# Queries and keys projected with dimensions on partitions, and heads gathered by SBUF transfers, in a hybrid attention layer

## What is computed

```python
h = einsum('bnd,de->bne', x, w_in)             # 1024 -> 3328 columns
qa, ka, va, ga, qb, kb, vb, gb = split(h)      # 512 each, but kb and vb 128
qa, ka = rope(qa), rope(ka)                    # mixer A: 8 heads, 1-D rotary
out_a = dilated_attention(qa, ka, va) * silu(ga)   # mask with multiplicities 0 to 3
qb = axial_rope(rms_norm_heads(qb, q_norm))    # mixer B: 8 query heads,
kb = axial_rope(rms_norm_heads(kb, k_norm))    # 2 key/value heads, 2-D rotary
out_b = softmax(qb @ kb.T * scale) @ vb * silu(gb)
f = concat(out_a, out_b) @ w_out
y = layer_norm(alpha * x + f) * ln_g + ln_b
```

## Time and profile before

| | |
|---|---|
| three runs | 474.97, 476.57, 477.52 us; median 476.57 |
| profiled execution, first to last instruction | 474.6 us |
| PE busy | 438.0 us, 92% |
| DVE, POOL, ACT busy | 301.4, 248.1, 230.7 us |
| DMA | 30.00 MB, mean 63 GB/s |

### The profile page before, as it was taken

One profiled execution on the slowest core, in us unless ns is written; L12 is line 12 of the kernel. 1 busy time (PEld: TensorE's weight loads), 2 busy tenths in 40 slices (PEclk: granted clock), 3 DMA queues, 4 the chain that ended last, 5 costly groups with the idle time before them and its releaser, 6 DMA issues.

```text
span 474.6 us, 8965 instructions
## 1 busy us (share of the span) xinstructions
PE 438.0 (92%) x3292; PEld 413.2 (87%) x3292; DVE 301.4 (64%) x826; ACT 230.7 (49%) x519; POOL 248.1 (52%) x340
## 2 busy tenths in 40 slices
PE   1999979998899999999999999999999789999990
PEld 1999969987799999998899999999888678999990
DVE  1543675339987788664577877855586777433664
ACT  3332113335456565666565565655675876121222
POOL 1126953795554746334346565653543773454664
PEclk9999989999899999999999999999999989999997
DMA  6611212110200101102010010110200136231222
GB/s 237 255 45 52 71 35 74 39 46 23 68 23 23 46 23 36 56 24 66 14 54 23 24 46 24 40 51 23 68 1 23 44 111 245 88 95 42 78 100 89
DMA packets 23291, 30.00 MB, mean 63 GB/s; under 512 B 1872, under 2 KB 19408, under 8 KB 23248
## 3 DMA queue, kind: packets, MB, share of 16 engines
q1 hardware_dynamic: 22816, 29.30, 19.0%
q10 hardware_dynamic: 432, 0.13, 0.1%
HBM read 26.28 MB, written 3.15 MB: 62 GB/s over the span
## 4 chain that ended last, share of the span: by engine, by line
PE 66%; POOL 10%; DVE 10%; issue 7%; ACT 3%; DMA 2%; SPq 1%; ACTq 0%; DVEq 0%; POOLq 0%
PE bank L504 15%; PE bank L505 15%; PE bank L506 15%; PE bank L465 9%; PE bank L593 6%; POOL scr L1062 3%; DVE prob L870 2%; PE bank L551 2%; PE bank L552 2%; DMA h<-x_prompt 2%; DVE tmp_s L796 1%; POOL tanh L1048 1%; ACT prob L707 1%; DVE p_lo L878 1%; POOL w_lo L1032 1%
## 5 line engine op out<-in xcount | busy, mean ns | idle before, releaser
L504 PE MATMUL bank<-w_hi,t_lo 128*128 128x256 f32 x576 | 168.2, 292 | 1.9 <-DVE nmax L870 0.8
L506 PE MATMUL bank<-w_hi,t_hi 128*128 128x256 f32 x576 | 164.0, 285 | 0.0
L505 PE MATMUL bank<-w_lo,t_hi 128*128 128x256 f32 x576 | 163.9, 285 | 0.0
L504 PEld LDWEIGHTS bank<-w_hi,t_lo 128*128 128x128 f32 x576 | 111.5, 194 | 3.1 <-DVE nmax L870 1.0
L505 PEld LDWEIGHTS bank<-w_lo,t_hi 128*128 128x128 f32 x576 | 111.6, 194 | 0.1
L506 PEld LDWEIGHTS bank<-w_hi,t_hi 128*128 128x128 f32 x576 | 111.3, 193 | 0.0
L1032 POOL TENSOR_TENSOR w_lo<-raw,w_hi 128x512 fp32r<-128x512 f32 x52 | 67.2, 1302 | 59.2 <-ACT w_hi L659 59.1
L1113 POOL TENSOR_SCALAR prob<-prob,den 128x512 f32<-128x512 f32 (+1 forms) x96 | 60.5, 635 | 68.6 <-DVE den L899 68.5
L707 ACT ACTIVATE prob<-prob,nmax 128x512 f32<-128x512 f32 (+1 forms) x96 | 62.3, 649 | 54.1 <-DVE nmax L870 53.6
L878 DVE TENSOR_TENSOR p_lo<-bank,p_hi 128x512 fp32r<-128x512 f32 x80 | 54.8, 685 | 3.0 <-ACT p_hi L716 2.2
L659 ACT ACTIVATE w_hi<-raw 128x512 fp32r<-128x512 f32 x62 | 37.6, 622 | 34.6 <-DMA raw<-w_in 17.4
(11 more groups left out here) (97 smaller groups left out, 784.3 us busy)
## 6 DMA issues: line engine op xcount, KB each, us to landing
raw<-w_in SPq DMA_DIRECT2D x50, 256.0 KB, 2.8
raw<-w_out SPq DMA_DIRECT2D x16, 256.0 KB, 2.9
h<-x_prompt SPq DMA_DIRECT2D x7, 512.0 KB, 6.8
h<-x_sample SPq DMA_DIRECT2D x4, 512.0 KB, 9.6
y_prompt<-h SPq DMA_DIRECT2D x8, 256.0 KB, 2.1
y_sample<-h SPq DMA_DIRECT2D x4, 256.0 KB, 2.1
cst<-consts SPq DMA_DIRECT2D x1, 960.0 KB, 9.5
h<-x_prompt SPq DMA_DIRECT2D x2, 256.0 KB, 3.8
```

Source lines behind the costliest of these rows:

```text
L504: nc.tensor.matmul(out, a_lo, b_hi, start=(m == 0), stop=False)
L505: nc.tensor.matmul(out, a_hi, b_lo, start=False, stop=False)
L506: ins = nc.tensor.matmul(out, a_hi, b_hi, start=False, stop=(m == KT - 1))
```

## The change

The layout of the data is redone on the host: x comes a second time, transposed (`xt`), the columns of `w_in` are permuted into 12 chunks and `w_out` into slices of one dimension block by 512 columns, all contiguous per partition. The first chunk (`START`) has 512 columns, the keys and queries of A's heads 0 to 3; the other 11 have 256.

- x is loaded transposed, 384 KB for a dimension block. There are no `x_transposes`.
- `start` projects the first chunk dimension block by dimension block, with six PSUM banks open, the weights stationary and the tokens streamed (512 and 256).
- Items are now 48 products of 256 columns (values and B's keys, two token tiles) or, for gates, B's queries and A's keys and queries, 24 of 512 columns (`n` = 0, 1) or 48 of 256 (`n` = 2).
- Queries and A's keys lie with dimensions on partitions, the first halves of four heads in one bank, the second halves in another. DVE multiplies by cosines and sines, POOL subtracts and adds two blocks of 768, ACT rounds 1536 columns, DVE takes the remainder.
- Each head is then gathered from these 32-partition pieces by DMAs from SBUF to SBUF: 4 for the queries of a head, 8 for its keys, 96 KB each. The per-head PE transposes are gone, but for 6 blocks of B's keys.
- B's queries get their RMS factor in `mask_max`; the sums of squares come from 24 products of 4 columns (`square_sums`).
- The output projection has 2 halves of 512 columns. Head order is A 0-3, B 0-7, A 4-7. Items end at step 64, 21 (block, tile) pairs of the output projection lie in steps 70 to 81, and 7 ring places hold the weights.

```diff
-ORDER = [10, 8, 11, 9, 12, 0, 2, 4, 6, 1, 3, 5, 7]
-BESIDE = ((0, 5), (3, 8), (55, 44), (62, 50), (65, 52), (72, 54))
+BESIDE = ([(c, n) for c in range(C_GA0, C_QB0 + 1) for n in range(3)] + [(KEYS_T, 0), (KEYS_T, 1)] +
+          [(c, n) for c in range(C_GB0, C_GA1 + 1) for n in range(3)])
+PACE = ((0, 0), (15, 9), (16, 11), (34, 17), (43, 20), (55, 29), (64, 32))
+WIDE_AT = {70: 0, 71: 1, 72: 2, 73: 3, 74: 4, 76: 5, 81: 6}
...
+                for n, src in enumerate((high[rows, 0], high[rows, 1], low[rows, 0], low[rows, 1])):
+                    sp.dma_start(q_st[32 * n:32 * n + 32, j % 4, :].bitcast(F32), src).then_inc(q_staged[j % 4], 16)
...
+                for part, src in enumerate((high, low)):
+                    for n in range(4):
+                        sp.dma_start(ka_st[32 * n:32 * n + 32, part, slot, :].bitcast(F32), src[rows, n % 2]) \
+                            .then_inc(ka_staged[slot], 16)
...
+            load_chunk(C_GA0)
+            sp.wait_ge(rot_lo, 1)
+            stage_keys(0)
+            sp.wait_ge(rot_lo, 2)
+            stage_query(0, "q")
+            for j in range(1, 4):
+                stage_keys(j)
+                stage_query(j, "q")
...
+            for c in range(C_VKB, C_QB1 + 1):
+                load_chunk(c)
...
+                for k in range(KT):
+                    pe.wait_ge(w_hi_done, k + 1)
+                    pe.wait_ge(x_hi, k + 1)
+                    for group in range(2):
+                        one(group, k, w_hi, t_hi, k == 0, False)
+                    pe.wait_ge(x_lo, k + 1)
...
+                nc.gpsimd.tensor_tensor(low[:, 0], low[:, 0], high[:, 1], ALU.subtract)
+                nc.gpsimd.tensor_tensor(low[:, 1], low[:, 1], high[:, 0], ALU.add).then_inc(rotated_done, 1)
```

More of the change, by code:

```diff
@@ L77 @@
+C_VA, C_GA0, C_VKB, C_QB0, C_GB0, C_QB1, C_GB1, C_KA1, C_VA1, C_QA1, C_GA1 = range(1, 12)
+KEYS_T = "keys"
+GATE_AT = {C_GA0: 0, C_GB0: 4, C_GB1: 6, C_GA1: 2}
+SLICE_W = 512
+SLICES_OF = [len(cols) * KT // SLICE_W for _, cols in CHUNKS]
+FIRST_SLICE = [sum(SLICES_OF[:c]) for c in range(len(CHUNKS) + 1)]
+IN_SLICES = FIRST_SLICE[-1]
+OUT_HALVES = D_MODEL // SLICE_W
+OUT_SLICES = OUT_HALVES * KT
+RING, RAW = 7, 2
+HEADS = N_HEADS_A + N_HEADS_B
 UNITS = QT + 1
@@ L234, in build @@
+        mix_hi, mix_lo = sem("mix_hi"), sem("mix_lo")
+        x_back = [sem(f"x_back{t}") for t in range(TILES)]
         ln_loaded = sem("ln_loaded")
@@ L454, in _ @@
+            for i in range(10, OUT_SLICES):
+                load_slice(IN_SLICES + i)
             for t in range(TILES):
@@ L541, in scores, with square_sums @@
+            def square_sums(item):
+                pe.wait_ge(products_done, square_items.index(item) + 1)
+                out = in_bank(index[item])
+                for t in range(4):
+                    ins = nc.tensor.matmul(out[:, 4 * t:4 * t + 4], sq[:, t * P:(t + 1) * P], pick, start=True, stop=True)
+                ins.then_inc(ssq_done, 1)
             def scores(u):
                 j, k = divmod(u, UNITS)
-                kv = head_columns(j)[4]
+                keys, slot = keys_of(j)
@@ L959, in _ @@
-            for item in alone:
-                after_projection(*item)
-            for b, item in zip(first, first_items):
-                t_low(b)
-                after_projection(*item)
+            for k in range(KT):
+                tokens_low(k)
+            dve.wait_ge(tab_k_loaded, 16)
+            dve.wait_ge(norm_loaded, 16)
+            after(nc.vector.tensor_tensor(tab_k[:, 0], tab_k[:, 0], norm_k[:, None, :].to_broadcast([P, QT, HEAD_DIM]),
+                                          ALU.mult))
@@ new lines, in _ @@
+                    if item[1] == 2 and item[0] in rot_chunks:
+                        rotate(item[0], 0)
+                if u == keys_end + 1:
+                    square_keys()
+                if u == keys_end + 2:
+                    key_power()
+                if u == keys_end + 4:
+                    add_keys()
+                for c in rotations_at(u - 2):
+                    if kind(c) == QUERY_B:
+                        query_power(c)
+                for i in OUT_SLICES_AT.get(u, ()):
+                    weights_low(IN_SLICES + i)
```

1400 lines of the change are left out of this document (704 added, 696 removed).

## The result

The changed kernel takes 512.3 us (median of 4 runs, 511.8 to 514.1) and the kernel before 476.9 beside it: the ratio is 1.077, with an interval of 1.073 to 1.080. The forecast was 458, faster. The change makes the kernel 7.7% slower.

The account below looks back on a forecast made before the run. PE, busy 92% of the span, was taken as the bound. Its work of 397.4 us plus start, waits, end and tail gave a 456.1 span; 2.0 for the median made 458, with a range of 443 to 474.

Parts of the forecast that it names:

- PE's work: Whole kernel: PE's products and transposes fall from 424.3 to 397.4 us, through wide products and fewer transposes.
- before unit 0: Beginning: PE starts at 6.9 us, loses 2 to the slow clock and 0.5 to the chain before first scores.
- first wait: Early units: slices 16 and 17 load behind gathers on SP's queue; PE idles 9.1 us, plus 2 for the clock.
- second wait: Step 20, B's first head: gathers and key copies come late; PE idles 4.9 us, plus 2 for the clock.
- the end: From step 64, without items: 20 steps paced by DVE and ACT take 54 us, with 14 idle for PE.
- tail: Behind the last product: 10.6 us as before, 0.6 more for wider statistics stores, 11.3 with slack.
- SP issues in 0.47 us each: SP's queue: each gather takes 0.47 us of issue, a price taken from 4 issues in 1.87 us.
- Rival 2: SP's queue: gathers occupy it beyond their issue; at 0.93 us each 480, each 0.1 us adding 4.8; chance 0.12.
- Smaller ones: Waits for sums of squares, about four times, 4 us; others, such as rotation of B's keys and stalls, 2 us.
- rival 3: Steps below 64 without an item: DVE, ACT or POOL can't follow, half of 33 cost 0.7 more, 470; chance 0.12.
- Rival 1: Gathers are hidden and neither forecast wait for late transfers appears: 18 us less, 440; chance 0.18.

Follow-up runs that it names:

- loads first: Changed kernel with all transfers kept, but loads of some weight slices, and B's first gathers, moved earlier on SP's queue: 486.8 us.
- before in threes: Kernel before, with its items between units 3 and 55 placed only in every third step, two or three at a time: 496.0 us (1.041).
- thirds: Against loads first: a head's keys in four transfers, and each item's products spread over up to two free steps ahead, in halves or thirds: 464.8 us.
- the moved rotation and square: POOL's rotation directly behind the next unit's scaling and ACT's square ahead of its slices, added to halved items (469.5 us) and to thirds (463.9).
- the moved rotation: Changed kernel with POOL's two rotation operations one and two steps later, ACT's and DVE's parts one step later: 524.4 us.
- all three edits: Against loads first: square ahead of ACT's slices and values ahead of sums, rotation behind the next unit's scaling, keys in four transfers: 484.0 us.
- the fourth step: Against loads first with keys in four transfers: a fifth probabilities buffer, so transposes come four steps behind scores instead of three: 485.7 us.

## Why the prediction was wrong

The sum was 456.1 for the span, and the span is 510.0. By its own terms, each measured on the changed kernel's profiled execution:

| term | forecast | measured |
|---|---|---|
| PE's work | 397.4 | 397.7 |
| before unit 0 (start, slow clock, handover) | 9.4 | 10.6 |
| first wait, clock included | 11.1 | 19.2 |
| second wait, clock included | 6.9 | 8.2 |
| squares, and everything else in units 11 to 63 | 4 + 2 | 42.9 |
| the end | 14 | 19.6 |
| tail | 11.3 | 11.6 |

- **PE's work, the beginning, the tail: right.** The first scores came at 60.5 us, where 60.1 was forecast, and the distances in wide items are those of the earlier trace rows (0.227 us in the item at 61.6 us).
- **The first wait: mechanism right, size off.** The step "SP issues in 0.47 us each" took the price of loads from HBM; these gathers take 0.63 (8 in 5.03 us). 48 x 0.16 = 7.7 us is how much later the slices' load came for it. PE stood from 74.0 to 90.3 us, where 73.4 to 82.5 was forecast. Rival 2's price of 4.8 us for each 0.1 holds too: 0.16 more, and the wait is 8.1 longer. Its condition, 0.93, was not reached, and the kernel was slower all the same.
- The Trainium skill's figure for transfers of 64 KB (DMA: Bandwidth & Descriptors, Measured) had given 0.71 us for a gather, an estimate. It was measured on loads from HBM issued by GpSimd, so it is another kind of transfer. The measured 0.63 is nearer to it than to my 0.47, which may be chance.
- **The second wait: right.** 6.3 idle and 1.9 of slow clock, where 4.9 and 2 were forecast.
- **The step that failed: "Smaller ones".** It counted the squares four times, which was nearly right (5.0 us in 5 waits), and 2 us for the rest, "as in the middle of before". All of it measured 42.9. The middle of before was no measure, as there an item or more stood between the transposes and the values of 38 of the 53 steps. The change makes items of 5.5 us out of items of 2.9 and leaves more than half the steps without one. In such a step PE has 0.9 to 1.8 us of work, where a step without items took 2.8 at the end of before. A long step doesn't give back what a short one loses: PE's time is then its own work, at full clock at best. I had all the numbers of this in rival 3: "half of the 33 steps", 0.7 us each, 12 us. I argued against it with DVE's busy share, and this was the mistake: DVE's work did fall and DVE is less busy. Its busy share doesn't tell whether a chain through it is late. The rival was right about where and wrong about how much. It left out the slow clock behind each wait (17 of the 51 us lost there), and waits for the squares, the rotation and late buffers. That short steps cost time is shown by the experiments; how the 42.9 us divide among these is not.
- **Rival 1, gathers hidden, 440:** with loads first they nearly were, and the time was 486.8. Of the difference between 440 and 487, 42 us are the middle again (47.8 where 6 were forecast).
- **The end: off by 5.6.** Waits of values for the low part as in the middle, with the slow clock at steps 66 to 70 (0.84 in the window of 388 to 410).

So two causes that were taken away one after the other hold 48 us of the changed kernel's time. Some 32 us are transfers in the wrong place and number, shown by 512.3 to 480.4. Another 16 are the size of the pieces, shown by 480.4 to 464.8 and, in direction, by before in threes. With both mended the change is worth 2.6%: the work saved by it was real all along. That 465 lies near the 458 forecast is no merit of the forecast, which had 18 us for two waits that the mended kernel doesn't have. Without them its sum is the 440 of rival 1. Of the 25 us above that, 19 lie in units 11 to 63, which still lose 24.7 with thirds where 6 were forecast, and 6 at the end (19.8 where 14 were). What the 24.7 consist of stays unsettled; the moved rotation and square didn't touch them.

## What to carry to other kernels

When a change makes larger the pieces of work that are put beside a chain of steps (here the items), count how many steps are left without one, and price each by the chain that then shows (here 2.8 us against 0.9 to 1.8) and the slow clock behind it. This is a first price and not the loss: before in threes has 30 such steps and loses only 13.5 us in units 11 to 63. A low busy share of the helpers is no argument that the loss is small. On one queue, ask of every transfer what is needed first, not what is ready first: here moving ten loads ahead of gathers was worth 25 us. And when a wait is removed and another takes its place, as with the moved rotation, with all three edits and with the fourth step, look at what could cover the waits, and not only at the operation that the list names.

## What the runs showed of the hardware

- Gathers from SBUF to SBUF of 32 partitions x 3 KB take 0.63 us of issue each, 8 in 5.03; loads of 256 KB from HBM 0.41, 2 in 0.81. In the kernel with one transfer of 128 partitions (384 KB) for a query, issues took 0.5 to 1.3 us in the first round, and the time from issue to landing was 4.2 us in the middle and 7.8 at most; for the gathers of the changed kernel it was 2.2 and 4.1.
- POOL's power operation takes longer with more columns: 4.18 us for 24, 2.29 for 12, 0.93 for 1, in rows of the changed kernel; a multiplication of 24 columns takes 0.24. One of the 24 stands behind each rotation of B's queries.
- What a wait costs behind it: in units 11 to 63 the rest, mostly products at the lower clock, is 17.2 us beside 33.9 of waits. The mean granted clock of the span is 0.983 before, 0.936 in the changed kernel, 0.969 with thirds. In the window of 160 to 200 us it is 0.87 where PE works 28.5 of 40 us.
